# Consecutive matmuls take turns between two accumulators

## The chip, the cores and the metric

One Trainium2 chip; the program uses one of its cores. The metric is the device time of one execution in microseconds (us). PE is TensorE, PEld its weight load, DVE VectorE, ACT ScalarE, POOL GpSimd, SP the engine that issues the weight transfers. A PSUM bank holds 512 float32 values in each of 128 partitions and is what a matmul accumulates into; there are eight, `bank0` to `bank7`.

## The reference

256 tokens of width 1024 pass through three blocks, all float32:

```
h = x
for i in range(2):
    u = rms_norm(h); h = h + (conformer_conv(u) if i == 0 else diff_attention(u))
    u = rms_norm(h); h = h + (silu(u @ w_gate) * (u @ w_up)) @ w_down     # width 2816
    h = h + sigmoid(rms_norm(h) @ ple_w_gate) * (p[i] @ ple_w_proj)
# then one more block: three gated branches a, b, c of 1024 columns each
proj = rmsnorm(h) @ w_in                                   # 1024 x 12288
merged = sum(sigmoid(gate_k) * (y_k @ w_branch_k) for k in (a, b, c))
out = rmsnorm(h + merged @ w_out)
```

Attention has 8 heads of two 64-wide halves, a relative bias, and a softmax for each half. Nearly all the arithmetic is in products of the 256 tokens with weight matrices.

## The kernel before

**Numbers in two parts.** A float32 operand is split into a high part rounded to the fp32r format and a low remainder (`x_hi` and `x_lo`, `z_hi` and `z_lo`, `w_hi` and `w_lo`). `mm3` makes one product of three matmuls into one accumulator: high by high (L254), high by low (L255), low by high (L256), each with a weight load of its own. The stationary operand is the first that `mm3` gets.

**Weights.** The 169 pieces of weights, 128 x 2048 each, arrive in a fixed order through a ring of four raw buffers. ACT makes `w_hi` (L761), DVE `w_lo` (L1176), in a ring of three slots. A piece's slot is free when PE has counted up `w_used`; PE waits for `lo_done` before a piece.

**Token-major chunks** (`token_chunk`, 60 of them). Tokens are stationary (128 at a time, so two tiles `t`), 512 columns of weights stream. A chunk is two pieces, the quarters `a = 0` and `a = 1` of its contraction of 8 x 128; each has four steps `k` for each of the two token tiles, so 24 matmuls in a quarter pair and 48 in the chunk. Token tile t has bank t. `begin(b)` waits until bank b was read out; `ready(a)` waits for the input of that quarter; `hooks[(a, t)]` are jobs that PE does after the matmuls of `(a, t)`, and `between` one after `a = 0`.

**Feature-major pieces** (`feature_piece`, 24 of them: 8 of `pw1`, 16 of `cc`). The weights are stationary, 256 tokens stream; a piece makes 2 x 128 features in the two halves `c` of one bank, 8 steps k of three matmuls for each half.

**Input of a chunk.** Where a stage needs the norm or product of a finished stage as input, PE transposes it (`transpose_job`, L296), in two halves n of 512 features, each with two jobs of four transposes. For the first of a stage, DVE multiplies with the gain (L1222), ACT rounds to the high part (L779), and DVE subtracts for the low part (L1232); for the branches ACT rounds (L798) and DVE subtracts (L1258) with no gain, in `wo` the same with L1002 and L1531. Quarter a needs half n = a. `later(m, 1)` puts the jobs of half 1 in `hooks[(0, 0)]` of the first chunk of `ffn0`, `ple0`, `q`, `ffn1`, `ple1` and `av`; `wo`, `wa`, `wb` and `wout` do the same with theirs. These ten chunks are "first chunks" below. In the chunks of attention, hooks carry transposes (`qk_jobs`, `weights`), and products of q and k (`logits`, L487).

**Order.** Each engine's program is an order written out by hand, and it runs in that order. PE has only the order below; DVE and ACT work through jobs of their own, and each waits for the others by semaphores.

Of the kernel before, what the change touches and what calls it, by code (L numbers as in the profile page):

```python
# [15 lines left out]
P = 128  # L16
SEQ, D = 256, 1024
TT = SEQ // P
KB = D // P
# [12 lines left out]
RAW, SPLIT = 4, 3  # L32
# [37 lines left out]
def build(nc, ws, x_tok, p_feat, par, rows, lam_rows, rel, onehot, sgu_w, pool_m, toep, out):  # L70
    ctx = ExitStack()
    with ctx:
        def sb(name, shape, dt=F32):
            return ctx.enter_context(nc.sbuf_tensor(name, shape, dt))

        def sem(name):
            return ctx.enter_context(nc.semaphore(name))

        raw = sb("raw", [P, RAW, HALF])
        w_hi = sb("w_hi", [P, SPLIT, HALF], F32R)  # L80
        w_lo = sb("w_lo", [P, SPLIT, HALF], F32R)
        h = sb("h", [P, TT, D])
        x_hi = sb("x_hi", [P, KB, SEQ], F32R)
        x_lo = sb("x_lo", [P, KB, SEQ], F32R)
# [10 lines left out]
        banks = [ctx.enter_context(nc.psum_tensor(f"bank{b}", [P, 512], F32)) for b in range(8)]  # L95
# [87 lines left out]
        hi_done, lo_done, w_used = sem("hi_done"), sem("lo_done"), sem("w_used")  # L183
# [43 lines left out]
        def _(pe):  # L227
# [4 lines left out]
            def begin(b):  # L232

                if released[b]:
                    pe.wait_ge(*released[b])

            def end(key, b, ins, piece=None, release=None):


                if release is None:  # L240
                    frees[b] += 1
                    release = (bank_free[b], frees[b])
                if piece is None:
                    ins.then_inc(pe_filled, 1)
                    count["filled"] += 1
                    filled[key] = (pe_filled, count["filled"], b, release)
                else:
                    ins.then_inc(w_used, 1)
                    filled[key] = (w_used, piece + 1, b, release)
                released[b] = release  # L250

            def mm3(dst, s_hi, s_lo, m_hi, m_lo, first, last):

                pe.matmul(dst, s_hi, m_hi, start=first, stop=False)  # L254
                pe.matmul(dst, s_hi, m_lo, start=False, stop=False)  # L255
                return pe.matmul(dst, s_lo, m_hi, start=False, stop=last)  # L256

            def tok(ap, k, t):
                return ap[:, k, t * P:(t + 1) * P]
# [5 lines left out]
            def token_chunk(key, g0, a_hi, a_lo, ready=None, between=None, release=None, hooks={}):  # L265

                for a in range(2):
                    if ready:
                        ready(a)
                    pe.wait_ge(lo_done, g0 + a + 1)  # L270
                    s = (g0 + a) % SPLIT
                    for t in range(TT):
                        b = t
                        if a == 0:
                            begin(b)
                        for k in range(4):
                            c = slice(k * 512, (k + 1) * 512)
                            ins = mm3(banks[b][:, :], tok(a_hi, 4 * a + k, t), tok(a_lo, 4 * a + k, t),
                                      w_hi[:, s, c], w_lo[:, s, c], a == 0 and k == 0, a == 1 and k == 3)
                        if a == 1:  # L280
                            end((key, t), b, ins, g0 + 1 if t == 1 else None, release(t) if release else None)
                        elif t == 1:
                            ins.then_inc(w_used, 1)
                        for step in hooks.get((a, t), ()):
                            step()
                    if a == 0 and between:
                        between()

# [15 lines left out]
            def h_release(m, n):  # L304
                return lambda t: (S("h_done"), 4 * m + 2 * n + t + 1)
# [6 lines left out]
            def ready_from(m):  # L312
                def ready(a):
                    wait_job((m, a, 0), (m, a, 1))
                return ready
# [17 lines left out]
            def feature_piece(key, g, b, release=None, ready=None):  # L333

                pe.wait_ge(lo_done, g + 1)
                begin(b)
                for c in range(2):
                    for k in range(KB):
                        if ready and c == 0 and k % 4 == 0:
                            ready(k // 4)  # L340
                        w = slice(k * 256 + c * P, k * 256 + (c + 1) * P)
                        ins = mm3(banks[b][:, c * SEQ:(c + 1) * SEQ], w_hi[:, g % SPLIT, w], w_lo[:, g % SPLIT, w],
                                  x_hi[:, k, :], x_lo[:, k, :], k == 0, k == KB - 1)
                end(key, b, ins, g, release)

            def later(m, n):

                return {(0, 0): [lambda: h_jobs(m, n)]}
# [112 lines left out]
            for f in range(KB):  # L461
                pe.wait_ge(S("y_sq"), f // 2 + 1)
                ins = pe.matmul(banks[7][:, 0:SEQ], inv_d, sq[:, f, :], start=f == 0, stop=f == KB - 1)  # L463
# [16 lines left out]
            def logits(hd):  # L480

                def go():
                    j, b0 = hd % 4, 4 + 2 * (hd % 2)
                    for c in range(2):
                        begin(b0 + c)
                        r = slice(c * HD, (c + 1) * HD)
                        pe.matmul(banks[b0 + c][:, 0:SEQ], q_f[r, j, P:SEQ], k_f[r, j, :], start=True, stop=True)  # L487
                        ins = pe.matmul(banks[b0 + c][:, SEQ:384], q_f[r, j, 0:P], k_f[r, j, 0:P], start=True, stop=True)
                        end(("lg", hd, c), b0 + c, ins, release=(S("lg_read"), 2 * hd + c + 1))
                return go  # L490

            def group_logits(hd):

                def go():
                    hg = hd // 4
                    wait_job(("qk", hg, 0, 0), ("qk", hg, 0, 1), ("qk", hg, 1, 0), ("qk", hg, 1, 1))
                    logits(hd)()
                return go
# [30 lines left out]
            def qk_jobs(hg, i):  # L529
                def go():  # L530
                    for t in range(TT):
                        transpose_job(("qk", hg, i, t), qk_t[:, i, t, :], (S("qk_normed"), 4 * hg + 2 * i + t + 1), False)
                return go

            g = G["qkv"]
# [3 lines left out]
                        hooks={(0, 1): [qk_jobs(0, 0)], (1, 0): [qk_jobs(0, 1)], (1, 1): [group_logits(0), logits(1)]})  # L539
            token_chunk(("k", 1), g + 6, x_hi, x_lo,  # L540
                        hooks={(0, 0): [logits(2)], (0, 1): [weights(0)], (1, 0): [logits(3)]})
            token_chunk(("v", 0), g + 8, x_hi, x_lo, release=lambda t: (S("v_copied"), t + 1),
                        hooks={(0, 0): [weights(1)], (0, 1): [qk_jobs(1, 0)], (1, 0): [weights(2)]})
            token_chunk(("v", 1), g + 10, x_hi, x_lo, release=lambda t: (S("v_copied"), t + 3),
                        hooks={(0, 0): [qk_jobs(1, 1)], (0, 1): [group_logits(4), logits(5)],
                               (1, 0): [weights(3), logits(6)], (1, 1): [weights(4), logits(7)]})
# [16 lines left out]
            for name in ("av", "au"):  # L563
                for n in range(2):
                    token_chunk((name, n), G[name] + 2 * n, x_hi, x_lo,
                                ready=ready_from(5) if name == "av" and n == 0 else None,
                                hooks=later(5, 1) if name == "av" and n == 0 else {})
# [3 lines left out]
            for t in range(TT):  # L571
                ins = pe.matmul(banks[4][:, t * P:(t + 1) * P], ones[:, :], diag[:, t, :], start=True, stop=True)
# [4 lines left out]
            for t in range(TT):  # L577
                for q in range(2):
                    b = 4 + 2 * t + q
                    begin(b)  # L580
                    for j in range(4):
                        gi = 4 * q + j
                        ins = pe.matmul(banks[b][:, j * P:(j + 1) * P], sgu_t[:, gi, :],
                                        av[:, t, gi * P:(gi + 1) * P], start=True, stop=True)
# [16 lines left out]
            for n in range(2):  # L601
                token_chunk(("wa", n), G["wa"] + 2 * n, z_hi, z_lo, ready=job_ready("ya") if n == 0 else None,
                            hooks={(0, 0): [y_jobs("ya", au, 1)]} if n == 0 else {})
# [9 lines left out]
            for f in range(KB):  # L613
                b = 4 + f // 2
                if f % 2 == 0:
                    begin(b)
                w = f // 2
# [3 lines left out]
                ins = pe.matmul(dst[:, P:SEQ], av[:, 1, fs], pm[:, w, SEQ:384], start=False, stop=True)  # L621
# [3 lines left out]
            g = G["poolw"]  # L625
# [3 lines left out]
            for n in range(2):  # L629
                for t in range(TT):  # L630
                    b = 4 * n + t
                    begin(b)
                    for w in (2 * n, 2 * n + 1):
                        for k in range(2):
                            c = slice((2 * w + k) * 256, (2 * w + k + 1) * 256)
                            ins = mm3(banks[b][:, (w % 2) * 256:(w % 2 + 1) * 256], tok(z_hi, 2 * w + k, t),
                                      tok(z_lo, 2 * w + k, t), w_hi[:, g % SPLIT, c], w_lo[:, g % SPLIT, c],
                                      k == 0, k == 1)
# [3 lines left out]
            for n in range(2):  # L642
                token_chunk(("wb", n), G["wb"] + 2 * n, z_hi, z_lo, ready=job_ready("yb") if n == 0 else None,
                            hooks={(0, 0): [y_jobs("yb", au, 1)]} if n == 0 else {})
# [13 lines left out]
            for n in range(2):  # L658
                token_chunk(("wout", n), G["wout"] + 2 * n, x_hi, x_lo, ready=job_ready("merged") if n == 0 else None,
                            hooks={(0, 0): [y_jobs("merged", merged, 1)]} if n == 0 else {},  # L660
                            release=h_release(6, n))
# [1215 lines left out]
```

## Time and profile before

| | |
|---|---|
| time, median of 3 runs | 1140.34 us (1139.01 to 1140.44) |
| span of the profiled execution, first to last instruction | 1138.6 us |
| PE busy | 1065.1 us of it |
| mean granted TensorE clock | 0.978 of full speed |
| matmuls | 5588, with 5588 weight loads |
| DVE busy, ACT busy | 726.4 us, 515.1 us |

A matmul's row gives its start and its length, but matmuls overlap: the next one starts before the last has ended. What PE sustains is the distance from start to start, which has to be read from rows that follow each other. The span is 1.7 us under the median of the runs.

### The profile page before, as it was taken

To read this page: it belongs to the slowest core of one execution; us is meant where nothing else is said; L and a number is where in the kernel's file an instruction comes from. 1 tells how busy PE (TensorE), PEld (TensorE's weight loads), DVE (VectorE), ACT (ScalarE), POOL (GpSimd) and SP (SyncE) were. 2 spreads that over 40 slices of the span, in tenths; PEclk is the share of its full clock that TensorE was granted. 3 is DMA by queue.
4 is the path that set the end of the run, shared out by engine and by line. 5 is a ranking of instruction groups with operands and counts; after the bars stand their busy time and mean duration, and the time that the engine had idled before them with its cause. 6 is when DMAs were issued, how large, how long until landed. Compare 5 with 4: busy or idle time off the path is not lost.

```text
span 1138.6 us, 13783 instructions
## 1 busy us (share of the span) xinstructions
PE 1065.1 (94%) x5588; PEld 906.7 (80%) x5588; DVE 726.4 (64%) x1006; ACT 515.1 (45%) x611; POOL 60.8 (5%) x65
## 2 busy tenths in 40 slices
PE   4989699999999929999999999999999999999996
PEld 3989587888887717877888888778888888999885
DVE  6899866455546727777644555777545465777555
ACT  4421165444444535676544444565454544443533
POOL 1066400000000000000000000000000000000000
PEclk9999799999999969999999999999999999999998
DMA  6521125555554654325655555355655445445530
GB/s 242 204 87 39 56 111 176 199 186 185 186 185 147 138 172 180 111 75 212 235 186 199 185 185 185 119 208 197 230 180 198 172 176 193 177 165 196 195 120 37
DMA packets 27438, 188.70 MB, mean 166 GB/s; under 512 B 3368, under 2 KB 3496, under 8 KB 5488
## 3 DMA queue, kind: packets, MB, share of 16 engines
q1 hardware_dynamic: 24912, 179.32, 44.0%
q0 software_dynamic: 2176, 8.05, 2.8%
q8 instruction: 44, 0.72, 0.2%
q10 hardware_dynamic: 288, 0.46, 0.1%
q14 instruction: 18, 0.15, 0.0%
HBM read 185.19 MB, written 2.62 MB: 165 GB/s over the span
## 4 chain that ended last, share of the span: by engine, by line
PE 77%; DVE 14%; DMA 5%; ACT 3%; issue 1%; POOL 0%; SPq 0%; ACTq 0%; DVEq 0%
PE bank L254 24%; PE bank L256 24%; PE bank L255 24%; DVE arena L1373 6%; DMA toep<-arena 3%; DVE w_lo L1176 2%; PE bank L296 1%; ACT w_hi L761 1%; PE bank L361 1%; DMA arena<-in_p_feat 1%; DVE x_lo L1232 1%; PE bank L463 1%; DMA h<-in_x_tok 0%; DVE arena L1222 0%; ACT x_hi L779 0%
## 5 line engine op out<-in xcount | busy, mean ns | idle before, releaser
L1176 DVE TENSOR_TENSOR w_lo<-raw,w_hi 128x2048 fp32r<-128x2048 f32 x169 | 386.6, 2291 | 227.3 <-ACT w_hi L761 226.8
L761 ACT ACTIVATE w_hi<-raw 128x2048 fp32r<-128x2048 f32 x169 | 322.3, 1909 | 165.7 <-PE bank L256 157.7
L254 PE MATMUL bank<-w_hi,x_hi 128*128 128x512 f32 x800 | 319.5, 399 | 27.9 <-ACT arena L952 22.0
L256 PE MATMUL bank<-w_hi,x_lo 128*128 128x512 f32 x800 | 313.8, 392 | 0.0
L255 PE MATMUL bank<-w_lo,x_hi 128*128 128x512 f32 x800 | 313.1, 391 | 0.0
L254 PEld LDWEIGHTS bank<-w_hi,x_hi 128*128 128x128 f32 x800 | 151.2, 189 | 64.3 <-issue 28.5
L256 PEld LDWEIGHTS bank<-w_hi,x_lo 128*128 128x128 f32 x800 | 151.0, 189 | 32.6
L255 PEld LDWEIGHTS bank<-w_lo,x_hi 128*128 128x128 f32 x800 | 151.4, 189 | 29.6
L254 PE MATMUL bank<-w_hi,z_hi 128*128 128x512 f32 (+1 forms) x368 | 142.9, 388 | 1.8 <-DVE z_lo L1418 0.9
L256 PE MATMUL bank<-w_hi,z_lo 128*128 128x512 f32 (+1 forms) x368 | 141.7, 385 | 0.0
L255 PE MATMUL bank<-w_lo,z_hi 128*128 128x512 f32 (+1 forms) x368 | 141.6, 385 | 0.0
L254 PE MATMUL bank<-x_hi,w_hi 128*128 128x256 f32 x384 | 110.0, 286 | 2.3 <-DVE x_lo L1232 2.3
L255 PE MATMUL bank<-x_lo,w_hi 128*128 128x256 f32 x384 | 109.8, 286 | 0.0
L256 PE MATMUL bank<-x_hi,w_lo 128*128 128x256 f32 x384 | 109.7, 286 | 0.0
L254 PEld LDWEIGHTS bank<-w_hi,z_hi 128*128 128x128 f32 x368 | 69.2, 188 | 16.4 <-DVE z_lo L1531 1.1
L256 PEld LDWEIGHTS bank<-w_hi,z_lo 128*128 128x128 f32 x368 | 69.1, 188 | 13.9
L255 PEld LDWEIGHTS bank<-w_lo,z_hi 128*128 128x128 f32 x368 | 69.2, 188 | 13.4
L254 PEld LDWEIGHTS bank<-x_hi,w_hi 128*128 128x128 f32 x384 | 74.9, 195 | 2.7 <-issue 2.7
L255 PEld LDWEIGHTS bank<-x_lo,w_hi 128*128 128x128 f32 x384 | 74.9, 195 | 0.0
L256 PEld LDWEIGHTS bank<-x_hi,w_lo 128*128 128x128 f32 x384 | 74.9, 195 | 0.0
L1373 DVE SCALAR_TENSOR_TENSOR arena<-arena,prm 128x256 f32<-128x256 f32 x120 | 66.9, 632 | 0.0
L806 ACT ACTIVATE z_hi<-bank 128x512 fp32r<-128x512 f32 x22 | 13.1, 595 | 75.7 <-PE bank L361 75.7
(211 smaller groups left out, 906.8 us busy)
## 6 DMA issues: line engine op xcount, KB each, us to landing
raw<-in_ws SPq DMA_DIRECT2D x169, 1024.0 KB, 4.8
arena<-in_rows POOLq DMA_DIRECT2D x2, 1024.0 KB, 6.0
toep<-arena POOLq DMA_DIRECT2D x1, 1536.0 KB, 36.9
h<-in_x_tok SPq DMA_DIRECT2D x2, 512.0 KB, 4.7
arena<-in_rows POOLq DMA_DIRECT2D x2, 512.0 KB, 3.8
arena<-toep POOLq DMA_DIRECT2D x1, 1024.0 KB, 7.9
out<-arena SPq DMA_DIRECT2D x2, 512.0 KB, 2.7
arena<-in_pool_m POOLq DMA_DIRECT2D x1, 768.0 KB, 4.4
```

The source lines that it names most:

```text
L254: pe.matmul(dst, s_hi, m_hi, start=first, stop=False)
L255: pe.matmul(dst, s_hi, m_lo, start=False, stop=False)
L256: return pe.matmul(dst, s_lo, m_hi, start=False, stop=last)
L296: ins = pe.transpose(banks[b][:, k * P:(k + 1) * P], src[:, k * P:(k + 1) * P], ident[:, :])
L361: ins = pe.transpose(banks[b][:, k * SEQ + t * P:k * SEQ + (t + 1) * P], hid[:, t, k * P:(k + 1) * P], ident[:, :])
L463: ins = pe.matmul(banks[7][:, 0:SEQ], inv_d, sq[:, f, :], start=f == 0, stop=f == KB - 1)
L761: act.activation(w_hi[:, g % SPLIT, :], raw[:, g % RAW, :], ACT.Copy).then_inc(hi_done, 1)
L806: act.activation(z_hi[:, k0:k0 + 2, :], bank[:, :].rearrange("p (k s) -> p k s", k=2), ACT.Copy).then_inc(S("t_hi"), 1)
L1176: dve.tensor_tensor(w_lo[:, g % SPLIT, :], raw[:, g % RAW, :], w_hi[:, g % SPLIT, :].bitcast(F32), ALU.subtract).then_inc(lo_done, 1)
L1232: dve.tensor_tensor(lo[:, k0:k0 + 4, w], stage[:, s, :].rearrange("p (k c) -> p k c", k=4), hi[:, k0:k0 + 4, w].bitcast(F32), ALU.subtract ...
L1373: ins = dve.scalar_tensor_tensor(out=y[:, f, :], in0=u_pad[:, f, tap:tap + SEQ], scalar=col("dw_w", f * TAPS + tap), in1=y[:, f, :], op0=A ...
```

## The change

In a feature-major piece the loop over the halves c becomes the innermost: each of the three products of a step k is made for half 0, then for half 1. Only the very first matmul into the bank starts an accumulation. In a token-major chunk the first quarter (`a == 0`) is made in another order: six matmuls into bank 0 (k = 0, 1), then twelve that alternate between bank 0 (k = 2, 3) and bank 1 (k = 0, 1), then six into bank 1 (k = 2, 3). The second quarter stays as it was. The hooks of `(0, 0)` and of `(0, 1)` both run after all 24 matmuls of the first quarter, and `begin(1)` comes after six matmuls in place of twelve.

```
-                    for t in range(TT):
-                        b = t
-                        if a == 0:
-                            begin(b)
-                        for k in range(4):
+                    if a == 0:
+
+                        def one(t, k, i):
                             c = slice(k * 512, (k + 1) * 512)
-                            ins = mm3(banks[b][:, :], tok(a_hi, 4 * a + k, t), tok(a_lo, 4 * a + k, t),
-                                      w_hi[:, s, c], w_lo[:, s, c], a == 0 and k == 0, a == 1 and k == 3)
-                        if a == 1:
-                            end((key, t), b, ins, g0 + 1 if t == 1 else None, release(t) if release else None)
-                        elif t == 1:
-                            ins.then_inc(w_used, 1)
-                        for step in hooks.get((a, t), ()):
-                            step()
+                            return pe.matmul(banks[t][:, :], tok(a_lo if i == 2 else a_hi, k, t),
+                                             (w_lo if i == 1 else w_hi)[:, s, c], start=k == 0 and i == 0, stop=False)
+
+                        begin(0)
+                        for k in (0, 1):
+                            for i in range(3):
+                                one(0, k, i)
+                        begin(1)
+                        for k in (0, 1):
+                            for i in range(3):
+                                one(0, 2 + k, i)
+                                one(1, k, i)
+                        for k in (2, 3):
+                            for i in range(3):
+                                ins = one(1, k, i)
+                        ins.then_inc(w_used, 1)
+                        for t in range(TT):
+                            for step in hooks.get((0, t), ()):
+                                step()
...
-                for c in range(2):
-                    for k in range(KB):
-                        if ready and c == 0 and k % 4 == 0:
-                            ready(k // 4)
-                        w = slice(k * 256 + c * P, k * 256 + (c + 1) * P)
-                        ins = mm3(banks[b][:, c * SEQ:(c + 1) * SEQ], w_hi[:, g % SPLIT, w], w_lo[:, g % SPLIT, w],
-                                  x_hi[:, k, :], x_lo[:, k, :], k == 0, k == KB - 1)
+                for k in range(KB):
+                    if ready and k % 4 == 0:
+                        ready(k // 4)
+                    for i in range(3):
+                        for c in range(2):
+                            w = slice(k * 256 + c * P, k * 256 + (c + 1) * P)
+                            ins = pe.matmul(banks[b][:, c * SEQ:(c + 1) * SEQ], (w_lo if i == 2 else w_hi)[:, g % SPLIT, w],
+                                            (x_lo if i == 1 else x_hi)[:, k, :], start=k == 0 and i == 0 and c == 0,
+                                            stop=k == KB - 1 and i == 2 and c == 1, skip_group_check=True)
```

PE, in the first chunk of `ffn0`, around the transposes of the second half of its input (from `h` into banks 2 and 3). Before, they stand between the twelve matmuls of bank 0 and the twelve of bank 1 of the first quarter:

```order
L256 MATMUL bank0<-w_hi,x_lo 128x512
L296 MATMUL bank2<-ident,h 128x128 [waits bank_free2,h_done]
L296 MATMUL bank2<-ident,h 128x128 x3
L296 MATMUL bank3<-ident,h 128x128 [waits bank_free3,h_done]
L296 MATMUL bank3<-ident,h 128x128 x3
L254 MATMUL bank1<-w_hi,x_hi 128x512 [waits h_done]
L255 MATMUL bank1<-w_lo,x_hi 128x512
```

Now they stand after all 24, and the next row is the second quarter, which waits for their split (`x_split`):

```order
L276 MATMUL bank1<-w_hi,x_hi 128x512
L276 MATMUL bank1<-w_lo,x_hi 128x512
L276 MATMUL bank1<-w_hi,x_lo 128x512
L314 MATMUL bank2<-ident,h 128x128 [waits bank_free2,h_done]
L314 MATMUL bank2<-ident,h 128x128 x3
L314 MATMUL bank3<-ident,h 128x128 [waits bank_free3,h_done]
L314 MATMUL bank3<-ident,h 128x128 x3
L254 MATMUL bank0<-w_hi,x_hi 128x512 [waits lo_done,x_split]
```

So twelve matmuls moved from behind the transposes to ahead of them.

PE, in the last chunk of attention (`v`, second group), at the transposes of the k vectors of the second group of heads, and the q by k products of head 4 (L487, L488). Before, twelve matmuls of bank 1 stand between the two:

```order
L296 MATMUL bank3<-ident,arena 128x128 x3
L254 MATMUL bank1<-w_hi,x_hi 128x512 [waits v_copied]
L255 MATMUL bank1<-w_lo,x_hi 128x512
L256 MATMUL bank1<-w_hi,x_lo 128x512
L254 MATMUL bank1<-w_hi,x_hi 128x512
L255 MATMUL bank1<-w_lo,x_hi 128x512
L256 MATMUL bank1<-w_hi,x_lo 128x512
```

Now the products stand right behind the transposes, and wait for the copies out of banks 2 and 3:

```order
L276 MATMUL bank1<-w_hi,x_lo 128x512
L314 MATMUL bank2<-ident,arena 128x128 [waits bank_free2,qk_normed]
L314 MATMUL bank2<-ident,arena 128x128 x3
L314 MATMUL bank3<-ident,arena 128x128 [waits w_copied,qk_normed]
L314 MATMUL bank3<-ident,arena 128x128 x3
L507 MATMUL bank4<-arena 128x256 [waits bank_free3,bank_free2,lg_read]
L508 MATMUL bank4<-arena 128x128
```

PE, at the start of the second chunk of a feed-forward block: the wait of bank 1 for the reader of the chunk ahead (`hidden`) now stands at the seventh matmul, in the middle of bank 0's:

```order
L276 MATMUL bank0<-w_hi,x_hi 128x512 [waits hidden,lo_done]
L276 MATMUL bank0<-w_lo,x_hi 128x512
L276 MATMUL bank0<-w_hi,x_lo 128x512
L276 MATMUL bank0<-w_hi,x_hi 128x512
L276 MATMUL bank0<-w_lo,x_hi 128x512
L276 MATMUL bank0<-w_hi,x_lo 128x512
L276 MATMUL bank0<-w_hi,x_hi 128x512 [waits hidden]
L276 MATMUL bank1<-w_hi,x_hi 128x512
L276 MATMUL bank0<-w_lo,x_hi 128x512
L276 MATMUL bank1<-w_lo,x_hi 128x512
```

Before, that wait stood at the thirteenth matmul.

## Rows read from the trace of the kernel before

**Rows 1.** The page, part 4: engines of the chain that ended last

```profile
PE 77%; DVE 14%; DMA 5%; ACT 3%; issue 1%; POOL 0%; SPq 0%; ACTq 0%; DVEq 0%
```

**Rows 2.** PE's waits: for whom, total us, times, longest

```profile
PE bank L254 <- ACT arena L952: 22.0, 1, 22.0
...
PE bank L254 <- DVE z_lo L1531: 0.7, 1, 0.7
```

**Rows 3.** Timeline of PE, bank 4 to 5 (`down`), and 27 on: start, length, instruction

```profile
209.36 0.39 PE L256 MATMUL bank<-w_hi,z_lo 128*128 128x512 f32 x1
209.59 0.39 PE L254 MATMUL bank<-w_hi,z_hi 128*128 128x512 f32 x1
...
215.48 0.39 PE L256 MATMUL bank<-w_hi,z_lo 128*128 128x512 f32 x1
```

**Rows 4.** Timeline of PE, first and last of the 768 matmuls of `cc`

```profile
970.03 0.28 PE L254 MATMUL bank<-x_hi,w_hi 128*128 128x256 f32 x1
...
1062.06 0.28 PE L256 MATMUL bank<-x_hi,w_lo 128*128 128x256 f32 x1
```

**Rows 5.** Timeline, first chunk of `ffn0`: transposes, following matmul, last low parts

```profile
176.29 1.03 PE L296 MATMUL bank<-ident,h 128*128 128x128 f32 x8
177.08 0.48 PE L254 MATMUL bank<-w_hi,x_hi 128*128 128x512 f32 x1
...
178.31 1.29 DVE L1232 TENSOR_TENSOR x_lo<-arena,x_hi 128x512 fp32r<-128x512 f32 x2
```

**Rows 6.** Timeline, first chunk of `ple1`: the same, with the second quarter's start

```profile
730.69 1.04 PE L296 MATMUL bank<-ident,h 128*128 128x128 f32 x8
...
733.22 1.29 DVE L1232 TENSOR_TENSOR x_lo<-arena,x_hi 128x512 fp32r<-128x512 f32 x2
...
734.62 0.47 PE L254 MATMUL bank<-w_hi,x_hi 128*128 128x512 f32 x1
```

**Rows 7.** Timeline, `av`: last matmul ahead of the transposes, low parts, second chunk's start

```profile
754.59 0.39 PE L256 MATMUL bank<-w_hi,x_lo 128*128 128x512 f32 x1
...
757.58 1.48 DVE L1232 TENSOR_TENSOR x_lo<-arena,x_hi 128x512 fp32r<-128x512 f32 x2
...
765.86 0.47 PE L254 MATMUL bank<-w_hi,x_hi 128*128 128x512 f32 x1 [0.73 <-ACT arena L1071]
```

**Rows 8.** Timeline, first chunk of `wa`: transposes, last low parts

```profile
850.02 1.03 PE L296 MATMUL bank<-ident,arena 128*128 128x128 f32 x8
...
851.36 1.29 DVE L1258 TENSOR_TENSOR z_lo<-bank,z_hi 128x512 fp32r<-128x512 f32 x2 [4.55 <-ACT z_hi L798]
```

**Rows 9.** Timeline, attention: ACT's copies out of banks, PE's job behind the second

```profile
470.19 0.49 ACT L980 ACTIVATE arena<-bank 128x384 f32<-128x384 f32 x1 [1.32 <-PE bank L508]
...
474.13 1.25 ACT L965 ACTIVATE arena<-bank,st 128x512 f32<-128x512 f32 x2
476.38 0.49 PE L508 MATMUL bank<-ident,arena 128*128 128x128 f32 x3
```

**Rows 10.** Timeline, second chunk of `ffn0`: its seventh matmul, bank 1's reader

```profile
186.71 0.39 PE L254 MATMUL bank<-w_hi,x_hi 128*128 128x512 f32 x1
...
187.41 0.48 DVE L1283 SCALAR_TENSOR_TENSOR arena<-bank,st,arena 128x256 f32<-128x256 f32 x1
```

**Rows 11.** Stretches: length, PE, PEld, DVE, ACT, POOL busy (instructions), granted clock

```profile
361.00:364.30 3.30, 1.66 (x7) 0.95 (x6) 3.20 (x6) 3.02 (x8) 0.00 (x0) 1.00 0.59 251
364.40:367.70 3.30, 3.30 (x10) 2.43 (x9) 1.80 (x11) 2.16 (x5) 0.00 (x0) 0.50 0.00 0
...
724.00:728.00 4.00, 1.62 (x12) 1.27 (x11) 3.51 (x7) 2.19 (x5) 0.00 (x0) 1.00 0.71 262
728.00:731.40 3.40, 3.40 (x19) 2.86 (x20) 2.32 (x11) 3.09 (x8) 0.00 (x0) 1.00 0.00 0
```

**Rows 12.** Timeline of PE in the slow stretch of rows 11

```profile
365.33 0.63 PE L255 MATMUL bank<-w_lo,x_hi 128*128 128x512 f32 x1
365.76 0.63 PE L256 MATMUL bank<-w_hi,x_lo 128*128 128x512 f32 x1
```

More of the change, by code:

```diff
@@ L271, in token_chunk @@
                     s = (g0 + a) % SPLIT
-                    for t in range(TT):
-                        b = t
-                        if a == 0:
-                            begin(b)
-                        for k in range(4):
-                            c = slice(k * 512, (k + 1) * 512)
-                            ins = mm3(banks[b][:, :], tok(a_hi, 4 * a + k, t), tok(a_lo, 4 * a + k, t),
-                                      w_hi[:, s, c], w_lo[:, s, c], a == 0 and k == 0, a == 1 and k == 3)
-                        if a == 1:
-                            end((key, t), b, ins, g0 + 1 if t == 1 else None, release(t) if release else None)
-                        elif t == 1:
-                            ins.then_inc(w_used, 1)
-                        for step in hooks.get((a, t), ()):
-                            step()
+                    if a == 0:
+                        def one(t, k, i):
+                            c = slice(k * 512, (k + 1) * 512)
+                            return pe.matmul(banks[t][:, :], tok(a_lo if i == 2 else a_hi, k, t),
[16 more added lines that the diff above has]
+                                step()
+                    else:
+                        for t in range(TT):
+                            for k in range(4):
+                                c = slice(k * 512, (k + 1) * 512)
+                                ins = mm3(banks[t][:, :], tok(a_hi, 4 + k, t), tok(a_lo, 4 + k, t),
+                                          w_hi[:, s, c], w_lo[:, s, c], False, k == 3)
+                            end((key, t), t, ins, g0 + 1 if t == 1 else None, release(t) if release else None)
+                            for step in hooks.get((1, t), ()):
+                                step()
```

## The prediction

> **What bounds the kernel now.** I read first the shares of the chain that ended last: PE has 77% of it, DVE 14%, DMA 5% [rows 1]. So a change to PE's program counts nearly one for one, wherever PE isn't waiting already. Then PE's waits: the largest is once 22.0 us, for ACT's copy at the start of the chunks of k [rows 2]; whatever PE does later ahead of it costs nothing as long as the chain behind that wait isn't late itself. Then the timeline of PE, for the distance from start to start. At 512 columns, 27 distances take 215.48 - 209.36 = 6.12 us, 0.227 each [rows 3]. The 768 matmuls of `cc`, 256 columns each, take 1062.06 - 970.03 = 92.03 us for 767 distances: 120.0 ns each [rows 4].
>
> **What alternating can give or take.** The change makes neighbours use different accumulators. The old order already has such neighbours. In [rows 3] the last matmul of bank 4 starts at 209.36, the first of bank 5 at 209.59: 0.23 us, the same as the average of the 26 inside bank 5 behind it, 0.227. In `cc`, 15 changes of bank and 16 of half lie in the 767 distances, which still average 120.0 ns [rows 4]. If matmuls into one accumulator waited for each other, switches would be shorter; if a switch cost something, they would be longer. Neither shows, to the 10 ns of a row. I take zero for it. The bounds are from the slow stretch: at a granted clock of 0.50, 1.2 GHz of the two levels [rows 11], starts are 0.43 us apart at 512 columns [rows 12], which is what 512 columns take at one per cycle, 0.427. At full clock the columns are then 213.3 ns, and 13.3 of the 227 are something else; for 256 columns 106.7 of 120.0, again 13.3. If that rest were a price of staying in one accumulator, alternating could take away 13.3 ns a pair at most. There are 46 new such pairs in each of 24 feature-major pieces (47 distances, of which one changed half before) and 10 in each of 60 token-major chunks (11 inside the twelve that alternate, less the one switch from bank 0 to bank 1 that was there before): 1104 + 600 = 1704. The bound is 22.7 us of gain.
>
> The Trainium skill, "TensorE: Matmul & The Clock Gate", section "Back-to-back issue gap", gives an isolated matmul N / 2.4 + 2.5 ns, 215.8 at N = 512 and 109.2 at 256, without regard to the accumulator. The trace has 227 and 120.0, 11 ns more each. Were the accumulator the reason, the sum would by that page be 11 x 1704 = 18.7 us lower (an estimate). The switches of [rows 3, 4], which show nothing of these 11 ns, are why the sum doesn't have it.
>
> **What moving the hooks costs.** In the old order PE transposes the second half of a stage's input behind the twelve matmuls of bank 0, and then has twelve of bank 1, 12 x 0.227 = 2.72 us, while DVE and ACT split it. Now the transposes stand behind all 24, and the next instruction is the second quarter, which waits for that split. Nothing on PE covers it. The 2.72 us of matmuls themselves are only moved.
>
> `ffn0` and `ffn1`: transposes start at 176.29, the matmul behind them at 177.08, 0.79 later; the last low part ends at 178.31 + 1.29 = 179.60, 3.31 after the transposes' start [rows 5]. The wake-up is 734.62 - 734.51 = 0.11 [rows 6]. Pause: 3.31 - 0.79 + 0.1 = 2.6 us each, 5.2 for both.
>
> `ple1`: already tight. The transposes start at 730.69 + 2.72 = 733.41, the split ends at 736.72, and the second quarter, at 734.62 before [rows 6], starts at 736.8: 2.2.
>
> `av`: the last matmul ahead starts at 754.59 and now 2.72 later, the transposes at 757.54, the split ends 3.31 after, at 760.85, where it was 757.58 + 1.48 = 759.06 [rows 7]. Its second chunk waits for ACT at 765.86, and that ACT job stands behind the same split, so it moves along: 1.8.
>
> `wa`, `wb`, `wout`: transposes at 850.02, low parts until 851.36 + 1.29 = 852.65, 2.63 later [rows 8]; less 0.79, plus 0.1: 1.95 each, 5.8. `wo` waits for its low parts already, 0.7 us [rows 2]; from nothing to 1.95, I take 1.0.
>
> `ple0` and `q` lie ahead of the wait of 22.0 us. Pauses between them and it are hidden; but what that wait follows (the bias's write and read by DMA) is started by DVE jobs that stand behind the transposed input, 2.7 us later than before. With the DMA's chain on the path (DMA has 5% of it, [rows 1]), 2.7.
>
> Attention's hooks: those of `(0, 0)` and `(0, 1)` now run back to back. In the first `v` chunk a copy by ACT that began 474.13 - 470.19 = 3.94 behind an earlier one [rows 9] now comes 2.72 later, is through with its first part (a little over half of 1.25) at 474.13 + 2.72 + 0.7 = 477.55, and PE's L508, at 476.38 before, wants the bank: 1.3 with the wake-up. In the second, the q by k products stand right behind the transposes and need ACT's two copies out of the banks; a pair takes 1.25 [rows 9]. Less what overlaps, 1.2. Together 2.5.
>
> The second chunk of a feed-forward block: bank 1's reader ends at 187.41 + 0.48 = 187.89; the wait stands now at the seventh matmul, which started at 186.71 [rows 10]: 187.89 + 0.1 - 186.71 = 1.28, twice 2.6. At the other chunk boundaries the reader of bank 1 is done 0.1 us or more before the seventh matmul; the bounds are 0 and 10 x 0.15, I take 0.
>
> Sum of the pauses: 5.2 + 2.2 + 1.8 + 5.8 + 1.0 + 2.7 + 2.5 + 2.6 = 23.8 us.
>
> **The clock behind the pauses.** In 361.00 to 364.30 PE is busy 1.66 of 3.30 us, and the next 3.30 run at 0.50; in 724.00 to 728.00 it is busy 1.62 of 4.00, and the clock stays at 1.00 [rows 11]. A stretch like the first costs 8 matmuls x (0.427 - 0.227) = 1.6 us. Of the eight new pauses of 1.8 to 2.6 us (two `ffn`, `ple1`, `av`, three branches, one of `wo` and attention) none at one end, all at the other, 0 and 12.8; I take three: 4.8.
>
> Span: 1138.6 + 23.8 + 4.8 = 1167.2. The profiled execution is 1.7 us below the median, so the forecast is 1168.9, say 1169, 2.5% slower.
>
> **Rivals.** *The pauses open, the distances stay* (above): 0.76, by its own range 1163 to 1174 (`wo` 0 or 1.95, the DMA's 2.7 there or not, the clock 0 to 8).
>
> *Each new pair of neighbours saves 11 to 13.3 ns*, because part of the 13.3 is the accumulator's. Against it stand the switches; for it, that a row shows 10 ns at best, and [rows 4] would hide 31 x 13 / 767 = 0.5 ns. So the one test that is sharp enough is missing, and I give it 0.10: 1168.9 - 18.7 to 22.7, 1146 to 1150. The version that ends on the other side is this one with the pauses' price below it: the saving must reach 23.8 / 1704 = 14 ns a pair for no change. That is just over the bound of 13.3 with no half clock at all, so it needs a smaller sum of pauses as well, by some 6 us; 0.03 of the 0.10, at 1134 to 1140.
>
> *Every long pause brings the half clock*: 12.8 in place of 4.8, 1177: 0.06.
>
> *The pauses are partly covered*, because DVE and ACT reach the transposed banks sooner when their other jobs were done in the 2.72 us before: the split would take less than 3.31. ACT and DVE work in order and have little else there, but in [rows 8] DVE waited 4.55 us before its low parts, so they are ready and only the chain of transposes, round, subtract is left. With half the price of the pauses, 1155: 0.05.
>
> *Alternation itself costs*: a few ns for each switch, 1704 x 3 = 5, and 1174 or more: 0.03.
>
> **Numbers.** 0.2% of the time, 2.3 us, is about what a measurement here can tell from no change. Faster by more than that: 0.03 from the second case and 0.01 for what I haven't seen. Same: 0.04, from the second and the fourth. Slower: 0.92. The range reaches down to half of the pauses and up to the half clock behind all of them: 1155 to 1178.
>
> **What would show it.** In the profile after: waits of PE for `x_lo` and `z_lo` at the second quarter of the ten first chunks, 1.8 to 2.6 us each, some 15 us in all; a wait at the seventh matmul of the second feed-forward chunk, 1.3; starts still 0.23 apart where bank 0 and bank 1 take turns, and 120 ns in `pw1` and `cc`, where no hook was moved and the span of 768 matmuls should stay 92.0; the mean clock a little below 0.978, and PE's busy time up only by the slow stretches. The forecast is wrong if 120.0 ns changes in `cc` (by 10 ns, 7.7 us there alone), if the first chunks' second quarters start without a wait, or if stretches at 0.50 stand behind each of them.

## The result and the profile after

| | before | after |
|---|---|---|
| time, median | 1140.11 us (1139.01 to 1140.44, 4 runs) | 1172.05 us (1167.42 to 1173.43, 4 runs) |
| ratio | | 1.0279 (1.0257 to 1.0300) |
| span of the profiled execution | 1138.6 us | 1170.0 us |
| mean granted clock | 0.978 | 0.969 |

The change costs 32 us; 1169 was forecast, in the range 1155 to 1178. On another chip it was 1173.10 against 1139.76, 1.0300 (1.0286 to 1.0314).

The page of the changed kernel, part 2, PE's busy share and clock in 40 slices, and part 4, the chain by engine, beside [rows 1]:

```profile
PE   4989698999998949999899999899999999999996
...
PEclk9999799999999969999999999899999999999999
...
PE 75%; DVE 14%; DMA 4%; ACT 4%; issue 2%; POOL 0%; SPq 0%; ACTq 0%; DVEq 0%
```

PE still leads the chain. Rows of its waits (for whom, us in all, times, longest), to be held against [rows 2] and the row of before that stands first here:

```profile
PE bank L254 <- DVE x_lo L1232: 6.3, 3, 2.4
```

```profile
PE bank L276 <- ACT arena L972: 17.4, 1, 17.4
...
PE bank L254 <- DVE x_lo L1252: 14.3, 6, 2.4
...
PE bank L276 <- DVE x_lo L1252: 4.0, 2, 2.4
PE bank L254 <- DVE z_lo L1278: 3.4, 2, 1.7
...
PE bank L276 <- DVE arena L1303: 2.1, 2, 1.1
PE bank L254 <- DVE z_lo L1551: 1.9, 1, 1.9
PE bank L254 <- DVE x_lo L1278: 1.7, 1, 1.7
```

L254 is now the first matmul of a second quarter, and 14.3 + 3.4 + 1.9 + 1.7 = 21.3 us stand at the ten first chunks (two of the six of 2.4 stand at `ple0` and `q`, ahead of the wait of 22.0, which has shrunk to 17.4). These rows are new. So is L276 for L1303, 2.1: the wait at the seventh matmul of the second feed-forward chunks. The 4.0 of L276 for `x_lo` isn't: these two waits, 1.65 ahead of `ple0` and 2.38 ahead of `ple1`, are part of the 6.3 of before, with 2.3 at the first matmul of `pw1`.

The timeline of the first chunk of `ffn0` (start, length, engine, instruction; x2 is two matmuls under one row), to be held against [rows 5]:

```profile
173.77 0.62 PE L276 MATMUL bank<-w_hi,x_hi 128*128 128x512 f32 x2
...
176.49 0.39 PE L276 MATMUL bank<-w_hi,x_hi 128*128 128x512 f32 x1
...
177.85 1.03 PE L314 MATMUL bank<-ident,h 128*128 128x128 f32 x8
```

The twelve that take turns need 176.49 - 173.77 = 2.72 us, 0.227 each, as matmuls into one bank did [rows 3]. Behind the transposes at 177.85 the next matmul starts at 181.27, 3.42 later, where it was 0.79. The 768 matmuls of `cc` run from 998.84 to the next chunk at 1091.00, beside [rows 4]:

```profile
998.84 0.40 PE L361 MATMUL bank<-x_hi,w_hi 128*128 128x256 f32 x2
...
1091.00 0.40 PE L276 MATMUL bank<-w_hi,x_hi 128*128 128x512 f32 x1
```

That is 92.16 us, 120.0 ns each, with every neighbour in the other half.

Where the 31.4 us of span came from, by when PE reaches the same place in the two timelines:

| up to | before | after | added |
|---|---|---|---|
| first chunk of `ffn0` | 173.46 | 172.33 | -1.1 |
| `ffn0`, hooks of its second chunk | 190.85 | 195.23 | 5.5 |
| first chunk of `ple0` | 363.20 | 367.56 | 0.0 |
| past the wait of the k chunk (hooks of `q1`) | 442.71 | 448.15 | 1.1 |
| `o` transposes, second block | 508.27 | 516.07 | 2.4 |
| first chunk of `ffn1` | 538.14 | 548.89 | 2.9 |
| `ffn1`, hooks of its second chunk | 555.54 | 571.74 | 5.4 |
| first chunk of `ple1` | 727.87 | 744.06 | 0.0 |
| end of `au` | 798.75 | 822.47 | 7.5 |
| first chunk of `wa` | 847.30 | 871.04 | 0.0 |
| first chunk of `wb` | 947.34 | 973.60 | 2.5 |
| `cc` | 970.03 | 998.84 | 2.5 |
| first chunk of `wout` | 1106.89 | 1135.70 | 0.0 |
| end of the span | 1138.6 | 1170.0 | 2.6 |

Nothing is added at the 1104 pairs of feature-major pieces. What is added lies at the moved hooks and the seventh matmul, and in the clock. The pause of `ffn0` and the stretch behind it, the stretches behind the pauses of `ple1`'s first chunk and of `av`, and the pause of `wa` with the stretch behind it (columns as in [rows 11]):

```profile
178.70:181.20 2.50, 0.19 (x2) 0.00 (x0) 2.40 (x5) 1.99 (x3) 0.00 (x0) 1.00 0.00 0
182.40:185.60 3.20, 3.20 (x9) 2.52 (x8) 2.24 (x1) 0.00 (x0) 0.00 (x0) 0.50 0.00 0
...
755.80:759.10 3.30, 3.30 (x10) 2.53 (x9) 3.30 (x2) 1.61 (x1) 0.00 (x0) 0.50 0.14 20
783.20:786.30 3.10, 3.10 (x9) 2.45 (x8) 2.69 (x4) 3.08 (x3) 0.00 (x0) 0.50 0.00 0
877.30:879.10 1.80, 0.22 (x2) 0.00 (x0) 1.28 (x2) 1.80 (x3) 0.00 (x0) 1.00 0.00 0
879.30:882.60 3.30, 3.30 (x15) 2.71 (x16) 2.57 (x2) 2.51 (x2) 0.00 (x0) 1.00 0.00 0
```

In `ffn0` PE is idle, DVE splits, and 1 us after PE is back it runs for 3.4 us at 0.50, 1.2 GHz. Behind the other pauses such a stretch begins between 0.3 us before PE is back and 1.4 us after. Six of them lie on the path and aren't in the profile of before (`ffn0`, `wo`, `ffn1`, two in `ple1`, `av`). None follows the shorter pauses of the branches, 1.96 us from the start of the last transpose to the start of the next matmul, where the others have 2.65 (`wo` 2.18).

One of the two in `ple1` doesn't belong to a moved hook. It stands behind the pause ahead of the stage (744.06), which is 2.65 us long in the kernel before as well. In the profile of before no slow stretch follows it [rows 11]; of the eleven kept profiles in which this pause isn't filled, nine have one, those of the third, fourth and fifth experiments among them.

### The profile page after: what moved, and what is told of

Same layout as the page of the kernel before. It is cut to its first block, busy times and chain, and to the rows that moved or that the text cites. A ratio compares the mean times of both kernels' runs of the same rounds, so it can differ in the third digit from the quotient of the medians.

```text
span 1170.0 us, 13783 instructions
## 1 busy us (share of the span) xinstructions
PE 1076.8 (92%) x5588; PEld 913.9 (78%) x5588; DVE 726.8 (62%) x1006; ACT 514.8 (44%) x611; POOL 60.2 (5%) x65
## 4 chain that ended last, share of the span: by engine, by line
PE 75%; DVE 14%; DMA 4%; ACT 4%; issue 2%; POOL 0%; SPq 0%; ACTq 0%; DVEq 0%
PE bank L276 27%; PE bank L254 12%; PE bank L256 12%; PE bank L255 12%; PE bank L361 9%; DVE arena L1393 6%; DMA toep<-arena 3%; DVE w_lo L1196 3%; ACT w_hi L781 1%; PE bank L314 1%; DVE x_lo L1252 1%; PE bank L381 1%; DMA arena<-in_p_feat 1%; PE bank L483 1%; ACT x_hi L799 0%
## 5 line engine op out<-in xcount | busy, mean ns | idle before, releaser
L254 PE MATMUL bank<-w_hi,x_hi 128*128 128x512 f32 x400 | 163.3, 408 | 16.0 <-DVE x_lo L1252 14.3
L276 PE MATMUL bank<-w_hi,x_hi 128*128 128x512 f32 x400 | 143.9, 401 | 25.0 <-ACT arena L972 17.4
L256 PE MATMUL bank<-w_hi,x_lo 128*128 128x512 f32 x400 | 159.8, 400 | 0.0
L255 PE MATMUL bank<-w_lo,x_hi 128*128 128x512 f32 x400 | 159.4, 399 | 0.0
L276 PE MATMUL bank<-w_hi,x_lo 128*128 128x512 f32 x400 | 141.1, 394 | 0.0
L276 PE MATMUL bank<-w_lo,x_hi 128*128 128x512 f32 x400 | 141.0, 393 | 0.0
L254 PE MATMUL bank<-w_hi,z_hi 128*128 128x512 f32 (+1 forms) x288 | 112.0, 389 | 5.3 <-DVE z_lo L1278 3.4
L276 PEld LDWEIGHTS bank<-w_hi,x_hi 128*128 128x128 f32 x400 | 75.8, 191 | 47.1 <-issue 22.7
L256 PE MATMUL bank<-w_hi,z_lo 128*128 128x512 f32 (+1 forms) x288 | 111.2, 386 | 0.0
L255 PE MATMUL bank<-w_lo,z_hi 128*128 128x512 f32 (+1 forms) x288 | 111.0, 385 | 0.0
L254 PEld LDWEIGHTS bank<-w_hi,x_hi 128*128 128x128 f32 x400 | 77.6, 194 | 33.1 <-DVE x_lo L1252 15.5
L276 PEld LDWEIGHTS bank<-w_hi,x_lo 128*128 128x128 f32 x400 | 75.9, 190 | 16.3
L276 PEld LDWEIGHTS bank<-w_lo,x_hi 128*128 128x128 f32 x400 | 76.3, 191 | 15.3
L361 PE MATMUL bank<-x_hi,w_hi 128*128 128x256 f32 x384 | 78.1, 285 | 2.3 <-DVE x_lo L1252 2.3
L361 PE MATMUL bank<-x_hi,w_lo 128*128 128x256 f32 x384 | 78.0, 285 | 0.0
L361 PE MATMUL bank<-x_lo,w_hi 128*128 128x256 f32 x384 | 77.9, 284 | 0.0
L254 PEld LDWEIGHTS bank<-w_hi,z_hi 128*128 128x128 f32 x288 | 54.6, 189 | 16.6 <-DVE z_lo L1278 3.8
```

The costliest lines, as they stand in the source:

```text
L276: return pe.matmul(banks[t][:, :], tok(a_lo if i == 2 else a_hi, k, t), (w_lo if i == 1 else w_hi)[:, s, c], start=k == 0 and i == 0, stop ...
L361: ins = pe.matmul(banks[b][:, c * SEQ:(c + 1) * SEQ], (w_lo if i == 2 else w_hi)[:, g % SPLIT, w], (x_lo if i == 1 else x_hi)[:, k, :], st ...
```

## The experiments

**One: the feature-major part alone.** The loop over c innermost in `feature_piece`, all else as before.

> The kernel before, with only the feature-major pieces changed (halves take turns; 1104 of the 1704 new pairs). Theory (taking turns is free, the late transposes cost everything): 1140 us within 1 us, starts 0.120 us apart. Rival (changing the accumulator has a price or a gain of its own, the late transposes have the rest): 1104/1704 of it shows here; a price of 10 ns a pair would give 1151, a saving of 10 ns 1129.

Measured: 1139.29 us against 1140.07, ratio 0.9999 (0.9990 to 1.0007). `cc` takes 1061.02 - 968.87 = 92.15 us. With 1104 pairs, an interval of 0.9 us either way is under 1 ns a pair: neither a price nor a saving.

**Two: the hooks alone.** Matmuls in the old order:

```
-                        for step in hooks.get((a, t), ()):
-                            step()
+                        for key_t in ((1, t),) if a == 1 else ((0, 0), (0, 1)) if t == 1 else ():
+                            for step in hooks.get(key_t, ()):
+                                step()
```

> The kernel before, matmuls in the old order, with only the hooks of (0, 0) moved behind all 24 matmuls of the first quarter. Theory (the uncovered split is the cost): all of the change except the wait at the seventh matmul of the second feed-forward chunks, 1.23 + 1.21 = 2.4 us, so 1172.0 - 2.4 = 1169.6, and the same pauses of 2.55 and 1.85 us. Rival (taking turns costs): 1140 or little above.

Measured: 1167.41 us (1165.59 to 1170.42), ratio 1.0246 (1.0230 to 1.0261). 27 of the change's 32 us are there without one pair that takes turns. Its waits:

```profile
PE bank L254 <- DVE x_lo L1233: 21.1, 10, 2.4
...
PE bank L254 <- DVE z_lo L1259: 3.4, 2, 1.7
```

21.1 is the 14.3 + 4.0 of the changed kernel, and 2.7 at `pw1`, where every version waits. The time is 2.2 us under the forecast. The profiled execution took 1168.75, 0.9 under it: it has no half clock behind the pauses of `ffn1` and `av`, where the changed kernel's has, but one ahead of the late transposes of `ple0`, where the changed kernel's has none. Why three of the four executions differ from it by 1.7 to 3.2 us, no profile shows.

**Three: take turns, with the hooks where they cover.** The changed kernel, `(0, 0)` behind the twelfth matmul:

```
                         for k in (0, 1):
                             for i in range(3):
                                 one(0, 2 + k, i)
                                 one(1, k, i)
+                            if k == 0:
+                                for step in hooks.get((0, 0), ()):
+                                    step()
```

> The changed kernel, with the hooks of (0, 0) back behind the twelfth matmul (in the middle of the twelve that take turns). Theory: twelve matmuls cover the split again, all pauses of 1.85 to 2.65 us go, the wait at the seventh matmul stays: 1140.1 + 2.4 = 1142.5 us. Rival (taking turns costs): about 1172.

Measured: 1142.43 us against 1140.07, ratio 1.0019 (1.0011 to 1.0028). The pairs take turns (but for those that a hook now parts), 2.4 us are left, and the profile has the wait for bank 1:

```profile
PE bank L276 <- DVE arena L1305: 2.1, 2, 1.1
```

**Four: the early wait alone.** `begin(1)` at the seventh matmul, everything else as before.

> The kernel before, with only the wait for bank 1 moved from the thirteenth to the seventh matmul of a chunk. Theory: 1.2 us of wait in the second chunk of each feed-forward block and nothing else: 1142.5 us. Rival (the short waits at other chunk boundaries add up, or the wait is absorbed): 1144, or 1140.

Measured: 1141.71 us, ratio 1.0016 (1.0004 to 1.0027). The same 2.1 us of wait, and no sign of the other chunk boundaries.

**Five: half the cover.** The hooks of `(0, 0)` behind the eighteenth matmul.

> The changed kernel, with the hooks of (0, 0) behind the eighteenth matmul: six matmuls (1.36 us) cover the split in place of none or twelve. Theory: each pause is shorter by 1.36 us than in the changed kernel (1.2 in the feed-forward blocks' first chunks, 0.5 in the branches'), with the wait at the seventh matmul still there: between 1142.4 (twelve) and 1172 (none), near 1150, and up to 1156 if stretches at half clock stand behind the shorter pauses too. Rival (no part of the price hangs on the cover): 1142 or 1172.

Measured: 1150.82 us against 1139.67, ratio 1.0102 (1.0086 to 1.0117). In `ffn0` the second quarter follows the last matmul of the first by 1.39 us, of which 0.99 is a wait, against 2.65 behind the last transpose with no cover:

```profile
181.12 0.47 PE L254 MATMUL bank<-w_hi,x_hi 128*128 128x512 f32 x1 [0.99 <-DVE x_lo L1253]
```

With twelve, six and no matmuls of cover the times are 1142.4, 1150.8 and 1172. The second step is the larger one: no stretch at half clock lies behind the short pauses, and five lie behind the long ones.

**Six and seven: the pause filled.** The changed kernel, with ten more matmuls behind the late transposes; their product in bank 7 is read by nobody:

```
+                        if key in (('gu', 0, 0), ('gu', 1, 0), ('ple', 1, 0), ('av', 0), ('wo', 0)):
+                            begin(7)
+                            for _ in range(10):
+                                pe.matmul(banks[7][:, :], tok(a_hi, 0, 0), flat(a_hi)[:, 0:512], start=True, stop=True)
```

> The changed kernel, with ten extra matmuls (2.27 us, into bank 7, whose contents nobody reads) put into the pause of the first chunks of ffn0, ffn1, ple1, av and wo, behind the late transposes. Theory (PE's idle time brings the half clock behind it): the second quarters start no later than before, as the split still takes 2.65 us, and the stretches at half clock behind these five pauses go, 5 x 1.7 = 8.5 us: 1163.5. Rival (the half clock comes at its own times, or the idle time doesn't matter): 1172.

Measured: 1167.76 us, ratio 1.0250 (1.0236 to 1.0264). For a sharper comparison it ran again, beside the changed kernel:

> The changed kernel itself, beside the next two, since its own runs spread from 1167.4 to 1173.4 us and the comparison of the filled pauses rests on it. If the spread is the number of pauses with a stretch at half clock behind them: again 1167 to 1173 with the longer times at the lower mean clock, median near 1171.

> The five filled pauses once more, on the same chip as the changed kernel: if the filled pauses keep the clock, 4 to 8 us below it and with less spread; if not, the same as it.

Measured on one chip: the changed kernel 1173.10 (1172.51 to 1173.63), filled 1167.97 (1167.23 to 1168.27). Fifty extra matmuls, and 5.1 us less. The changed kernel's spread of its first runs didn't come again. In the profile of the first filled run PE is busy through the pause of `ffn0`, and the clock stays (the pause and the 3.3 us behind it, columns as in [rows 11]):

```profile
177.70:180.30 2.60, 2.60 (x14) 1.89 (x12) 2.50 (x5) 1.92 (x3) 0.00 (x0) 1.00 0.00 0
180.40:183.70 3.30, 3.26 (x15) 2.74 (x15) 2.35 (x3) 1.22 (x2) 0.00 (x0) 1.00 0.00 0
```

The timeline there:

```profile
177.02 1.03 PE L318 MATMUL bank<-ident,h 128*128 128x128 f32 x8
177.81 2.54 PE L298 MATMUL bank<-x_hi 128*128 128x512 f32 x10
180.44 0.47 PE L254 MATMUL bank<-w_hi,x_hi 128*128 128x512 f32 x1
```

The second quarter starts 3.42 us behind the transposes' start, as it did without filler. All five slow stretches are gone, and still the gain is 5.1 and not 8.5, for two reasons. Two of the five had hidden other waits: in the second chunk of `wo` the filled kernel waits 0.4 us for `h` (and its ten matmuls outlast the pause there by about 0.2), and behind `av` it waits for ACT at its second chunk. The changed kernel has neither wait:

```profile
783.84 0.47 PE L276 MATMUL bank<-w_hi,x_hi 128*128 128x512 f32 x1 [0.97 <-ACT arena L1095]
```

And both filled profiles have a slow stretch at the start of `ple0`, ahead of its late transposes, where both profiles of the changed kernel have none. The first filled run:

```profile
365.10:368.30 3.20, 3.16 (x8) 2.51 (x9) 2.19 (x9) 3.05 (x7) 0.00 (x0) 0.50 0.00 0
```

It makes the write of the bias 1.7 us later (11.72 us behind the first matmul of `ple0` in the second filled profile, 10.06 in the changed kernel's of the same chip), and with it the end of the wait ahead of the k chunks.

**Eight: seven pauses and two more filled.**

> The changed kernel with filler in the pauses of ffn0, ple0, q, wo, ffn1, ple1 and av (ten matmuls each) and in the two pauses ahead of ple0 and ple1 (18 transposes each). Theory (idle time brings the half clock): one to two us below the five filled ones, near 1165, with no stretch at half clock between ple1 and the end; what is left above 1140 are the pauses themselves, some 24 us. Rival: no difference to the five.

Measured: 1163.12 us (1162.23 to 1165.05), 10.0 under the changed kernel measured beside it, and 4.9 under the five, where 1 to 2 were expected. Its profile has none of the slow stretches at the start of `ple0` and of `ple1` that both profiles of the five have; that is worth some 3.3 us. Between the first block and the end only the one around the wait ahead of the k chunks is left, and the mean clock is 0.984. What is left above the kernel before is 23.4 us: the pauses without the clock. (The kernel before gains 1.8 by the same filler, below, so the like-for-like figure is 25.3.)

**Nine: more cover than before.** The kernel before, `(0, 0)` of first chunks behind the sixth matmul.

> The kernel before, with the hooks of (0, 0) of the ten first chunks behind the sixth matmul in place of the twelfth, so that 18 matmuls cover the split. Theory: only what still waited can be won: 0.3 in ple1, up to 0.9 behind av, 0.3 in wo, and 1.36 by the bias's earlier write ahead of the k chunks: 1137 to 1139 us. Rival (the transposes' own input isn't there so early and PE waits for it): 1141 or more.

Measured: 1140.56 us, ratio 1.0009 (1.0000 to 1.0019): a miss. Nothing was won, and it lies just under the rival's 1141. In `q` PE now waits for the transposes' own input, and the same in `wo` and `av`:

```profile
389.90 0.66 PE L299 MATMUL bank<-ident,h 128*128 128x128 f32 x4 [1.37 <-DVE h L1320]
```

**Ten: the kernel before, its own pauses filled.** `keep_warm(18, 0)` ahead of the first chunk of both `ple` stages.

> The kernel before, with 18 extra transposes of the identity (1.96 us, into bank 0, unread) in the pause ahead of ple0 and ple1. Theory: the half clock behind these two pauses goes (1.55 us in ple0, by way of the bias's write; in ple1 in the executions that have it): about 1138. Rival: 1140, if the clock isn't set by the pause, and 1141 or more if the extra transposes delay the chunk.

Measured: 1137.85 us (1136.98 to 1139.28, 11 runs) against 1139.67, ratio 0.9987 (0.9978 to 0.9995). The stretch behind the pause, at 0.50 in [rows 11], is now

```profile
364.40:367.70 3.30, 3.30 (x21) 2.79 (x20) 2.19 (x12) 2.22 (x6) 0.00 (x0) 1.00 0.02 5
```

This is the one version whose interval lies below the kernel before, by 0.13%.

**Eleven: the two together**, with the sixth matmul in the `ple` stages alone.

> The kernel before, with the extra transposes ahead of ple0 and ple1, and the hooks of (0, 0) behind the sixth matmul in these two stages alone, where an earlier run gained and PE didn't wait for the transposes' input. Theory: the bias's write starts 1.36 us earlier again and ple1's wait of 0.3 goes: 1.6 below the run with the extra transposes alone (1137.85), so 1136.2. Rival (the wait ahead of the k chunks ends by something else): 1137.8.

Measured: 1138.18 us, ratio 0.9992 (0.9983 to 1.0001): the rival's number. DVE's own chain for the norm factor (L1193 to L1195 in the tenth experiment's kernel) reaches its last step at 367.1 to 367.2 in both of the last two, and the multiply follows 0.1 us later, whether the transposes start at 365.00 or at 366.32. In the run without the earlier hooks:

```profile
366.32 1.04 PE L296 MATMUL bank<-ident,h 128*128 128x128 f32 x8
...
367.14 0.16 DVE L1193 TENSOR_TENSOR st<-st 128x2 f32<-128x2 f32 x1
367.22 1.29 DVE L1223 TENSOR_TENSOR arena<-bank,prm 128x512 f32<-128x512 f32 x2
```

## Why the prediction was right, term by term

**Taking turns: 0 forecast, 0 found.** The distances are 0.227 and 0.120 us as before, and the first and third experiments, each known to about 1 us over 1104 and 1704 pairs, bound a price or a saving to about 1 ns a pair (the third less the 2 us of the fourth, which has the same wait and no pairs). The Trainium skill, "TensorE: Matmul & The Clock Gate", "Back-to-back issue gap", gives for the isolated matmul a distance 11 ns shorter than the trace has. The trace doesn't agree with the page there, and whatever those 11 ns are, they are not the accumulator's.

**The first chunks.** `ffn0` and `ffn1`: 3.42 - 0.79 = 2.6 each, as forecast. `ple1`: the wait of 2.54 in place of one of 0.30, 2.2 as forecast. `av`: in the filled kernel, where the clock doesn't blur it, PE reaches the second quarter 1.4 us later (the old order already waited 0.7 between its transposes) and the second chunk 0.4 more: 1.8 as forecast. `wo`: the step between nothing and 1.95 was set at 1.0. From the chunk's start to its second quarter PE takes 529.31 - 520.84 = 8.47 us in place of 520.19 - 513.04 = 7.15, 1.3 more. The stretch at half clock behind it adds 1.6, and hides the 0.4 for `h` that the filled kernel shows. So the waits are worth 1.7: mis-sized. The 0.7 of [rows 2], the prediction's reason to take less than 1.95, was no reason: that wait stands at the first quarter, and it is there after the change too (0.7 at 520.84).

**The branches: 1.95 each forecast, 2.5 measured.** The wait of the second quarter is 1.85, and a second one follows, 0.51 in `wa` and `wb` and 0.57 in `wout`, that no term had. DVE's timeline in `wa` after the change:

```profile
877.82 1.29 DVE L1278 TENSOR_TENSOR z_lo<-bank,z_hi 128x512 fp32r<-128x512 f32 x2 [7.29 <-ACT z_hi L818]
880.03 4.49 DVE L1196 TENSOR_TENSOR w_lo<-raw,w_hi 128x2048 fp32r<-128x2048 f32 x2 [0.93 <-ACT w_hi L781]
884.44 1.28 DVE L1661 TENSOR_TENSOR arena<-bank,arena 128x512 f32<-128x512 f32 x2
```

DVE stands idle for 7.29 us in front of the low parts (4.55 before, [rows 8]), with the two weight splits queued behind them; these then push bank 0's reader to 884.44, and the next chunk waits for that bank. ACT's rows show the same. It stands idle in front of its late rounding of the input, and the rounding of the two next weight pieces, which DVE's splits need, is behind that in its program:

```profile
877.12 1.08 ACT L818 ACTIVATE z_hi<-bank 128x512 fp32r<-128x512 f32 x2 [5.19 <-PE bank L314]
878.09 3.72 ACT L781 ACTIVATE w_hi<-raw 128x2048 fp32r<-128x2048 f32 x2
```

The prediction named what waits on PE for the late split, but not what is queued behind it on ACT and DVE.

**The bias's write: 2.7 forecast, 1.1 measured.** The write is issued at 377.64 in place of 372.14, 5.5 later, of which 4.4 were late already. The transposes moved by 2.72 us, but in the kernel before, a stretch at half clock stood ahead of them [rows 11] and had delayed them by 1.5; after the change the stretch falls behind them. The term was right about the chain and took its start from a timeline with a delay of its own in it. Where the slow stretch stands ahead of the late transposes too, as in the second experiment's profile, the write comes 377.87 - 366.18 = 11.69 us behind the first matmul of `ple0`, against 372.14 - 363.20 = 8.94 before: 2.75, the forecast's 2.7.

**Attention: 2.5 forecast, 2.4 measured**, and the seventh matmul 2.6 and 2.4. In `v`'s second group the products wait for ACT's copies, and the chain is the one of the prediction:

```profile
492.22 1.27 ACT L985 ACTIVATE arena<-bank,st 128x512 f32<-128x512 f32 x2 [3.00 <-PE bank L314]
...
493.74 0.71 PE L507 MATMUL bank<-arena 64*128 64x256 f32 x4 [1.12 <-ACT arena L985]
```

**The sum and the clock.** The waits sum to 5.2 + 2.2 + 1.8 + 7.6 + 1.7 + 1.1 + 2.4 + 2.4 = 24.4 us, where 23.8 was forecast. That the sums are so close is in part luck: 2.5 too little for `wo` and the branches and 1.6 too much for the bias's write nearly cancel. The run with filled pauses says 23.4 to 25.3. The clock was the term that was too small: three stretches, 4.8 us, were forecast, six came, and 31.4 - 24.4 = 7.0 us (8.1 without the 1.1 gained at the start, where by the distances from start to start the kernel before ran the first 5.7 us of `pw1` at half clock and the changed one 3.4). That is less than 6 x 1.6, since the stretches behind `av` and `wo` cover waits. So the forecast of the added span, 28.6, was 2.8 low, 2.2 of it the clock's. The three was a choice between none and eight and not a reading. Its one support was that the clock stays up behind the pause ahead of `ple1` [rows 11], and in nine of eleven profiles it doesn't: one execution couldn't tell.

The rival that ends on the other side, a saving of 14 ns a pair, is refuted by the third experiment; that "every long pause brings the half clock" is nearly what happened: in both profiles of the changed kernel behind each of the seven pauses of 2.65 us and behind `wo`'s 2.18, but not behind the one of 2.13 ahead of `ple0` (which has it in the kernel before), nor behind the three of 1.96. In the second experiment three of the seven long ones had none, so it isn't certain for each. By its own sign of being wrong, a stretch at 0.50 behind each of the ten first chunks, the prediction holds, but with seven of the ten not by much.

## What to carry to other kernels

When an order of matmuls is changed, ask first what the moved block was hiding: here 2.7 us of matmuls stood between a transpose and the use of its result, and their place was worth some 22 us of waits, in ten first chunks and in attention, and most of the clock's 7, while the new pattern of accumulators was worth nothing. If two accumulators must take turns, keep the jobs for other engines in the middle of the first quarter, as the third experiment does, and look at what is queued behind the late job on those engines. A pause of PE costs more than its length when a slow stretch follows, and whether one follows is not to be read from one execution; useless matmuls in it pay if their operands and bank are free.

## What was not expected of the hardware

Fifty matmuls of extra work made the kernel 5.1 us faster, and with further filler in four more pauses 10.0, by the clock alone. And a stretch at half clock isn't always worth its 1.6 us: behind `av` it hid a wait of 1 us that came back when the clock was held, while ahead of the transposes of `ple0` it delays the bias's write, and with it all that waits for that. Why a pause of 2.65 us is followed by half clock in most executions and not in all was not settled.
